# RWKV stage: values turned once in the projection, bonus products summed in the output stage, and the bodies dealt anew

## What is computed

```python
z = token_shift(h @ w_in)                     # keys k, values v, queries r, low-rank rows
for d in range(2):                            # forward and backward in time
    kd = heads(k_dir[:, :, d])
    s_fin, ys = rwkv_scan(decay[d], kd, v, kk, a[d], r, s0[d], d == 1)
    outs.append(ys)
    bonuses.append(jnp.sum(r * kd * r_k, axis=-1, keepdims=True) * v)
o = head_group_norm(outs[0] + outs[1]) + (bonuses[0] + bonuses[1])
y = (o * silu(gate)) @ w_out
```

## Time and profile before

| what | value |
|---|---|
| median of 3 runs | 4964.72 us (4956.97 to 4971.5) |
| the profiled execution | 4968.32 us, its span 4966.4 us, mean granted clock 0.97 |
| project1 | about 2368 to 3014 us of the span |
| rwkv | about 3020 to 4689 us |
| merge1 | about 4691 us to the end |
| busy over the span | PE 93%, DVE 54%, ACT 36%, POOL 28% |

### The profile page before, as it was taken

The page is one execution under the profiler, slowest core; times in us unless marked ns, Lnnn a source line. Parts: engine busy times, 40 slices in busy tenths (PEclk is TensorE's granted clock), DMA queues, the critical chain, the costliest instruction groups (busy, mean ns, idle before and its releaser), DMA issues. The chain is left out here.

```text
span 4966.4 us, 120707 instructions
## 1 busy us (share of the span) xinstructions
PE 4625.1 (93%) x48510; PEld 2742.7 (55%) x48510; DVE 2674.7 (54%) x4780; ACT 1796.5 (36%) x4413; POOL 1378.9 (28%) x2884
## 2 busy tenths in 40 slices
PE   6999996999999999899999997999998999999699
PEld 3666663333333333454444444787777778878544
DVE  2444443655666654232143345766666667666476
ACT  1222221444444343033122223555555555555332
POOL 1111111323322331000000002555555455555343
PEclk8999997999999999899999998999999999999799
DMA  5222223000000002533412235677676666777575
GB/s 215 94 85 98 85 77 127 4 25 24 25 25 24 25 6 96 218 136 114 117 62 65 76 94 154 173 185 176 167 181 166 166 174 169 188 175 174 150 228 177
DMA packets 938529, 585.99 MB, mean 118 GB/s; under 512 B 659125, under 2 KB 882997, under 8 KB 923960
## 3 DMA queue, kind: packets, MB, share of 16 engines
q1 hardware_dynamic: 851514, 556.33, 38.3%
q10 hardware_dynamic: 86528, 22.82, 2.1%
HBM read 382.11 MB, written 196.88 MB: 117 GB/s over the span
## 5 line engine op out<-in xcount | busy, mean ns | idle before, releaser
L934 PE MATMUL at_bS<-at_qT,at_kT 97*64 97x512 f32 (+1 forms) x2368 | 607.0, 598 | 15.1 <-ACT at_pT L1032 14.5
L1645 PE MATMUL p_bU<-keep_hT,p_slab 128*128 128x512 f32 (+1 forms) x1504 | 591.3, 554 | 12.8 <-DMA p_slab<-in_o_w_in_dram 7.4
L1069 DVE TENSOR_REDUCE at_mx<-at_bM 128x1 f32<-128x512 f32 (+1 forms) x656 | 394.2, 628 | 353.8 <-PE at_bM L899 352.9
L2268 PE MATMUL rw_bank<-keep_rw_hg,rw_slab 128*128 128x256 f32 x2048 | 486.8, 392 | 22.4 <-DMA keep_rw_hg<-scratch_hT 22.4
L1032 ACT ACTIVATE at_pT<-at_bS 128x512 f32<-128x512 f32 (+1 forms) x592 | 342.5, 591 | 398.2 <-PE at_bS L934 378.8
L1645 PEld LDWEIGHTS p_bU<-keep_hT,p_slab 128*128 128x128 f32 x1504 | 286.6, 191 | 311.0 <-issue 282.7
L2268 PEld LDWEIGHTS rw_bank<-keep_rw_hg,rw_slab 128*128 128x128 f32 x2048 | 385.9, 193 | 88.9 <-DMA keep_rw_hg<-scratch_hT 24.9
L856 POOL TENSOR_TENSOR at_sum_pool<-at_sum_pool,at_pT 128x512 f32<-128x512 f32 x192 | 244.2, 1272 | 372.1 <-ACT at_pT L1032 354.7
L2052 POOL TENSOR_TENSOR rw_g_at<-rw_g_at,rw_g_prod 64x14 f32<-64x14 f32 (+6 forms) x1008 | 320.1, 318 | 79.0
L2050 POOL TENSOR_TENSOR rw_g_prod<-rw_g_at 64x14 f32<-64x14 f32 (+6 forms) x1008 | 310.7, 308 | 79.1
L934 PEld LDWEIGHTS at_bS<-at_qT,at_kT 97*64 97x64 f32 x2368 | 155.5, 137 | 279.8 <-issue 187.5
(11 more groups left out here) (288 smaller groups left out, 9624.5 us busy)
## 6 DMA issues: line engine op xcount, KB each, us to landing
keep_wide<-scratch_heads SPq DMA_DIRECT2D x144, 512.0 KB, 4.6
keep_rw_hg<-scratch_hT SPq DMA_DIRECT2D x64, 1024.0 KB
keep_gate<-scratch_inverses SPq DMA_DIRECT2D x576, 64.0 KB
scratch_bv<-keep_wide SPq DMA_DIRECT2D x144, 128.0 KB
scratch_products<-rw_NB SPq DMA_DIRECT2D x288, 64.0 KB
scratch_y<-rw_ysb ACTq DMA_DIRECT2D x288, 64.0 KB, 2.9
scratch_heads<-p_z SPq DMA_DIRECT2D x17, 1024.0 KB, 4.9
m_yin<-scratch_y SPq DMA_DIRECT2D x32, 512.0 KB, 5.6
```

What stands on the lines that cost most here:

```text
L934: last = pe.matmul(bS[rows, g % 3, 0:nq * P], kT[:, s, k * P + VH * x:k * P + VH * x + VH], qT[:, s, q0 * P:(q0 + nq) * P], start=True, st ...
L1069: nc.vector.tensor_reduce(mx[:, j, piece:piece + 1], bM[:, (FIRST_ITEM[b] + i) % 2, 0:n], AX.X, ALU.max).then_inc(max_red, 1)
L1645: last = pe.matmul(bU[:, n % 4, 0:w], slab[:, i, k, :], hT[:, k, tok:tok + w], start=(k == 0), stop=(k == KD - 1))
L2268: last = pe.matmul(DENSE[:, GT * half:GT * (half + 1)], slab[:, half, q, :], hg[:, x.slot, q, :], start=(q == 0 and half == 0), stop=(q == ...
```

## The change

Values are no longer turned in each body. `project1` turns a pair's values while the next pair's blocks run (18 transposes a pair through bank `bS`, five copies on VectorE, four stores) into a new scratch `vt`; `load_values` fetches them turned, and `load` fetches three features. The product `r * kd * r_k` is stored as it is (`bq`), and the output stage adds the two directions, sums over heads with `same` and multiplies by the values. The bodies' lists are dealt anew; `weights`, `queries` and `removal_keys` move to the body before. TensorE's and VectorE's loops over pairs in project1 become unrolled. The diff, cut to its core:

```diff
@@ project1, sync: after kk of pair p, the turned values of pair p-1
+                def store_values(p):
+                    sp.wait_ge(vt_out, NS * p + NS)
+                    for e in range(2):
+                        for h in range(2):
+                            to = W["vt"][row, HP * h:HP * h + HP].rearrange("a s (q e v) -> e (a s) q v", e=2, v=C)[e]
+                            sp.dma_start(to, vt[HP * e:HP * e + HP, :, HP * h:HP * h + HP]).then_inc(vt_st, 16)
@@ project1, tensor
+                def turn_values(p, x):
+                    if x == 0:
+                        pe.wait_ge(z_done, 3 + 2 * p + 2)
+                        pe.wait_ge(root, NS * (p + 1))
+                    if x == 4:
+                        pe.wait_ge(vt_out, NS * p + 1)
+                    for j, tile in enumerate(range(4 * x, min(4 * x + 4, NT))):
+                        col = tile * P + (0 if tile < NC_CTX else L0 - CTX)
+                        last = pe.transpose(bS[:, x % 4, j * P:(j + 1) * P], z[:, 0, col:col + P], keep["ident"][:])
+                    last.then_inc(vt_mm, 1)
@@ project1, tensor, the loop
-                with pe.Fori(0, PAIRS) as p:
+                for p in range(PAIRS):
-                    blocks(0, base, 0, 0)
+                    for b in range(NB):
+                        blocks(0, base, b, b, b + 1)
+                        if p and b:
+                            turn_values(p - 1, b - 1)
...
+                        if p and b == 0:
+                            turn_values(p - 1, 4)
...
+                for x in range(NS):
+                    turn_values(PAIRS - 1, x)
@@ project1, vector: five copies ahead of the keys' taps of the next pair
+                    if p:
+                        for x in range(NS):
+                            values_out(p - 1, x)
-                    shift_taps(1, 1, bass.ds(p, 1), 3 + 2 * p, links)
+                    shift_taps(1, 1, slice(p, p + 1), 3 + 2 * p, links)
...
+                for x in range(NS):
+                    values_out(PAIRS - 1, x)
@@ rwkv, sync
+                def load_values(m):
+                    if m.since(KEEP):
+                        sp.wait_ge(s_mm, 4 * (m.n - KEEP) + 4)
+                    for d in range(2):
+                        sp.dma_start(Vt[:, m.kept, d].rearrange("p c v -> p (c v)"), W["vt"][m.pair, :, span(tokens(m, d), GT)]).then_inc(v_l[m.kept], 16)
@@ rwkv, sync, body
                     spread(n.on(2))
+                    load_values(n.on(3))
                     dense_behind(n)
@@ rwkv, tensor, body: the new list up to the second chunk
+                    values(n, 0)
                     higher_orders(n, 1)
-                    values(n, 0)
                     higher_orders(n, 0)
                     open_r1(n, 0)
-                    bonus(n.on(3))
+                    open_state(n, 0)
+                    scores(n.on(3), 0, 0, 0)
                     removed(n, 0)
-                    open_state(n, 0)
                     low_rank(n.on(4))
                     close_state(n, 0)
                     turn(n.on(3), 1)
...
                     dense(dense_of(n), 0)
                     scores(n.on(3), 0, 1, 0)
+                    far_p(n.on(1), 1)
+                    scores(n.on(3), 0, 1, 1)
                     removed(n, 1)
+                    turn(n.on(3), 0)
                     open_state(n, 1)
...
                     dense(dense_of(n), 1)
                     close_state(n, 3)
-                    turn(n.on(4), 2)
@@ rwkv, scalar, body: the new list up to the second chunk, then its end
+                    take_r1(n, 0)
+                    turned(n.on(2), 0, 1, 0)
+                    turned(n.on(2), 0, 1, 1)
+                    take_sa(n, 0)
+                    rates(n.on(4), 0, 0)
+                    rates(n.on(4), 1, 0)
+                    rates(n.on(4), 1, 1)
+                    turned(n.on(3), 1, 0, 0)
+                    store_y(n.on(-1), 1)
+                    turned(n.on(3), 1, 0, 1)
+                    rates(n.on(4), 0, 1)
+                    take_y(n, 0)
+                    take_r1(n, 1)
+                    key_factors(n.on(4))
+                    store_y(n.on(-1), 0)
+                    turned(n.on(3), 1, 1, 0)
+                    turned(n.on(3), 1, 1, 1)
+                    take_sa(n, 1)
...
                     take_y(n, 3)
-                    store_y(n, 0)
@@ merge1, tensor
+                def head_sums(t):
+                    pe.wait_ge(bs_done, t + 1)
+                    pe.wait_ge(bv_done, t)
+                    for j in range(2):
+                        last = pe.matmul(bB[:, j, :], same[:], bsum[:, 4 * j:4 * j + 4, :].rearrange("p k t -> p (k t)"), start=True, stop=True)
+                    last.then_inc(hs_mm, 1)
...
                     if next1:
+                        head_sums(t + 1)
                         turn(t + 1, 1 - s)
@@ merge1, vector: merge
+                    v.wait_ge(hs_mm, t + 1)
+                    nc.vector.tensor_tensor(bv[:].rearrange("p k t -> p (k t)"), bB[:].rearrange("p j c -> p (j c)"),
+                                            vT[:, s].rearrange("p k t -> p (k t)"), ALU.mult).then_inc(bv_done, 1)
-                    nc.vector.tensor_tensor(mT[:], nT[:], bsum[:], ALU.add).then_inc(m_done, 1)
+                    nc.vector.tensor_tensor(mT[:], nT[:], bv[:], ALU.add).then_inc(m_done, 1)
```

More of the change, by code:

```diff
@@ L1598, in pair @@
                             sp.dma_start(heads[:, 2, 0:CTX], kk[:, 0:CTX]).then_inc(kk_st, 16)
-                with sp.Fori(0, PAIRS - 1) as p:
+                            if not (isinstance(p, int) and p == 0):
+                                store_values(p - 1)
+                pair(0, True)
+                with sp.Fori(1, PAIRS - 1) as p:
                     pair(p, True)
@@ L1887, in load @@
                     if d == 0:
-                        sp.wait_ge(tr_mm[2], m.n - 1)
+                        for one in (kd_done, b0_done, q_done):
+                            sp.wait_ge(one, m.n - 1)
                         sp.wait_ge(ar_done, 2 * m.n - 2)
@@ L2096, in low_rank @@
                     last.then_inc(lora_mm, 1)
-                def bonus(m):
-                    if not m.real:
-                        return
-                    if m.n == 0:
-                        pe.wait_ge(c_l, 16 * 10)
-                    pe.wait_ge(q_done, m.n + 1)
-                    if m.since(1):
-                        pe.wait_ge(sc_out, 4 * m.n)
-                    pe.matmul(bank[BONUS_AT][:], same[:], q[:].rearrange("p d t -> p (d t)"), start=True, stop=True).then_inc(bon_mm, 1)
                 def turn(m, i):
@@ L2519, in bonus_queries @@
                     v.wait_ge(kd_done, m.n + 1)
-                    v.wait_ge(bon_mm, m.n)
-                    nc.vector.scalar_tensor_tensor(out=q[:], in0=zin[:, m.two, :, 2, :], scalar=par[:, m.pair, 6:7], in1=kd[:],
+                    if m.since(2):
+                        v.wait_ge(q_st[m.two], 16 * (m.n - m.two))
+                    nc.vector.scalar_tensor_tensor(out=q[:, m.two], in0=zin[:, m.two, :, 2, :], scalar=par[:, m.pair, 6:7], in1=kd[:],
                                                    op0=ALU.mult, op1=ALU.mult).then_inc(q_done, 1)
@@ L2527, in removal_keys @@
                         return
+                    v.wait_ge(in_l[m.two], inputs_loaded(m))
                     v.wait_ge(ea_done, 2 * m.n + 2)
@@ L2830, in _ @@
                 project(0, 0)
+                head_sums(1)
                 turn(1, 1)
```

194 lines of the change are left out of this document (100 added, 94 removed).

## The result

The changed kernel takes 4981.08 us (median of 12 runs, 4969.07 to 4988.89), the kernel before 4966.97 (12 runs): ratio 1.0029, 95% interval 1.0018 to 1.004. I had forecast 4924 and a range to 4975; my own bounds with all ends one way had reached 4984. The profiled execution of the changed kernel has a span of 4973.5 us and took 4975.48.

A forecast was written before the change was run, and what follows sets the result against it. TensorE's list was taken to bound all three stages. Recurrence -95, projection +26 and output stage +28 gave -41 from 4968.3, so 4927.3, and 3.6 lower for the median: 4924 us, range 4865 to 4975.

The forecast's parts named there:

- What TensorE sheds, 1.92 us a body: Recurrence: values' transposes (0.59 us) and bonus head sum (1.33) leave each of 72 bodies, 138 us.
- A wait of 0.5 us at the keys' turn: Recurrence: TensorE's turn waits for ScalarE's last copy of the turned removal keys, 0.5 us a body, 36 us in all.
- The rest of the list looks clean: Recurrence: apart from the keys' turn, the new lists bring no further wait in bodies with dense work.
- rival B: Recurrence: a loop beside TensorE, such as SyncE, stops the body at 20.9 us, saving 0.7; 4969 us, chance 0.17.
- The seams, -13: Recurrence's seven two-body seams: SyncE's extra issues eat part of the gain; of 2.8 us about 1.8 stays.
- SyncE hidden in regular bodies: Recurrence: SyncE's round grows by 1.3 to 18.9 us but stays under the new body of 20.2.
- Projection, +19 for the pairs: Second projection: transposes and a longer wait for squares, 2.7 us for seven pairs; its uncovered end +7, together +26.
- Output stage, +28: Output stage: two head sums a tile add 1.72 us, plus late bonus sums at the start; period 16.4 us.
- Rival A: Recurrence: no wait at the turn and TensorE's idle time halves, 4845 us, or 4880 with the first only; chance 0.22.
- rival D: Second projection: TensorE's clock falls behind each clump of transposes, +24 us for each of seven pairs; 5094, chance 0.02.
- Rival C: Recurrence: slow store_y issues on ScalarE, 2.22 us a pair, make the turn wait 2.4 us; 5054, chance 0.09.
- theory S: From the experiments: TensorE's code arrives late, small products running off before the next block is there.

The follow-up runs named there:

- hg_once: Changed kernel without the hidden groups' loads after the first two, so dense work runs on stale groups: 4960.22 us, 0.9972.
- best: Changed kernel, second dense half split, hidden group loaded one body earlier, turned values' stores issued before the wait for the next pair's keys: 4935.71 us, 0.9936.
- ballast: Changed kernel with one more 512-column product a body ahead of the first scores, its sum thrown away: 5038.93 us, 1.0137.
- pad64: Changed kernel with 16 products of 2 columns (64 records) ahead of the recurrence's list on TensorE: 4992.3 us, 1.0042.

## Why the prediction was wrong, by its steps

- **What TensorE sheds, 1.92 us a body: right as far as its own work goes.** A gap-free regular body kept TensorE busy for 21.45 to 21.6 us before and for 19.6 after (few bodies after the change are free of gaps).
- **A wait of 0.5 us at the keys' turn: wrong, to the good.** 4.0 us in 1300, none in regular bodies. In the rows above ScalarE's four DMA issues, 0.6 us each, run beside its copies and rates (an issue from 4329.42 to 4330.03, a copy from 4329.57 to 4329.93); I had added them one after the other.
- **"The rest of the list looks clean": the step that failed.** It looked only at semaphores and put waits without one at nothing. TensorE's code comes in blocks, 4.26 us from one to the next where it was late, and the change makes the lists denser without making them much shorter: 1008 records a body in place of 1020, in 19.6 us of work in place of 21.5. Gaps rose from 36.0 to 80.2 us in 1300, which is 55 us over the stage's 1621. This is rival B's shape, a body that stops at 20.9 and saves 0.7 (21.26 and 1.07 in the profiled execution, 50 us in the recurrence as B had), but not its mechanism: neither SyncE nor the traffic is the limit of a regular body (`hg_once`).
- **The seams, -13: wrong in sign, +6.4.** The hidden group lands late, behind 1 MB of slabs (27.3 us of waits in 1300, 11.1 before); that dense work comes sooner in the shorter body is the likely reason, not a tested one. The load one body earlier takes 22.4 us off the seams here, where TensorE then waits for the slabs, and 20.7 us in the kernel before. That the old seams were bound by it too I had seen ("something beside TensorE limits there") and put down to SyncE's issues.
- **SyncE hidden in regular bodies: right** as far as the runs go.
- **Projection, +19 for the pairs: +16.0, right.** Its end, +7: mis-sized, +15.3. I counted issues and copies, and missed that one tile serves two pairs, so the last copies wait for the landing of stores that SyncE issues late. `best` takes 5.3 of it back.
- **Output stage, +28: +25.8, right**, with the period at 16.33.
- **Slips in the sums.** Rival A's 4880 leaves out the 7 us of the seams that its 4845 counts; by its own terms it is 4888. And the range ends at 4975 though the bounds reach 4984; the 4981.08 measured lie between.
- **The rule on transposes and the clock (rival D): no sign of it.** The granted clock is 1.00 in the projection's window with 18 transposes a pair, the upper level of 2.4 GHz. **Rival C**, a slow `store_y`: not seen at the turn. **Rival A** was not reached by the changed kernel.

In sum, from TensorE's waits in 1300 us: 44 more in gaps, 16 more for the late group, 11 more for VectorE's masks (L2189, in the first body of a seam, which has no dense half as cover), 11 less for ScalarE and VectorE otherwise: 61 us, or 76 over the stage. Of the 138 us shed, 62 are left by that, against 50.0 measured; 12 us I could not find in these views.

On equal terms, with the early group in both, the change costs 17 us by the ratios (1.0 against 0.9966; the two intervals leave 8 to 26). With its dense work dealt anew and its stores moved it gains 15 (4935.71 against 4950.76, one session; 0.9936 against 0.9966).

**Still open.** How many blocks of code TensorE holds ahead, and why the lists before the change lose less: the stretch from the first half's end to the second's start lasts 7.3 to 7.5 us in gap-free bodies of both kernels (after the change only two bodies of the whole trace are free of gaps there), and only the other stretch shrank, from 6.7 to some 4.85 us. That a fuller other stretch would give the fetch a lead was only argued, and `ballast`, which fills it again, left the gaps at 90 us; so this part of theory S stands unproved. The traces show one more difference: with 1008 records, four blocks almost exactly, a gap of the changed kernel stays at nearly the same place of the list body after body, while before, with 1020, its place moves by some 12 records a body. No run tests whether that matters.

## What to carry to other kernels

Where an engine runs hundreds of short instructions between long ones, count records per microsecond: in the two places read above a block of 254 records ran off in 2.8 us and the next came 4.26 us after it had begun, and TensorE stood still for the rest. Work taken off such a list counts in full only where the code keeps up; spread the long instructions instead, but ask of each which eviction or mask it covers before it is moved. An "issue" gap inside a batch that waits for nothing is the sign to look for, and padding by a fraction of a block is the test. An "issue" row ahead of an instruction that does wait can be a load whose landing the view did not name, as at the dense work here: compare it with the landings before it is booked as code.

## Not expected of the hardware

- Code comes in packets of 16 KB (3.90 MB in 238), one for 252 to 254 records of TensorE; TensorE goes on 2.2 us after the packet's start in the two places read above.
- With the DMA rate cut from 179 to 138 GB/s the gaps in the code were 91 us in place of 80 (102 with the waits for the slabs): the fetch did not get faster with less traffic.
- Shifting the code by 64 records, a change of no data, moved seven gaps by that many records to another batch (`pad64`); the time moved by no more than the noise (1.0042 against 1.0029).
